# FFN up-projections: the weights' high part times the high and low activations as one product of 512 columns, halves added afterwards

## The reference

```python
def conv_gated_mlp(hn, w_up, conv_w, conv_b, w_down):        # FFN 0 and 1
    u = causal_dwconv(hn @ w_up, conv_w, conv_b)
    gate, val = jnp.split(u, 2, axis=-1)
    return (jax.nn.silu(gate) * val) @ w_down
...
f = (jax.nn.silu(h @ w_ffn_gate[l]) * (h @ w_ffn_up[l])) @ w_ffn_down[l]   # FFN 2
```

## Time and profile before

| | |
|---|---|
| median of 3 runs | 1277.9 us (1277.18 to 1284.03) |
| profiled execution | 1283.02 us, its span 1281.2 us |
| PE busy | 1201.9 us, 94% |
| PE weight loads | 1084.9 us, 85% |
| DVE busy | 721.3 us, 56% |
| ACT busy | 705.4 us, 55% |
| POOL busy | 883.3 us, 69% |
| granted TensorE clock, mean | 0.987 |

### The profile page before, as it was taken

How to read it: one execution, slowest core, us unless ns; L and a number is a source line. 1 busy time by engine, 2 the same in 40 slices (tenths; PEclk the granted TensorE clock), 3 DMA queues, 4 the chain that set the end, 5 groups by cost and what they waited for, 6 DMA issues and landing times.

```text
span 1281.2 us, 23414 instructions
## 1 busy us (share of the span) xinstructions
PE 1201.9 (94%) x8140; PEld 1084.9 (85%) x8140; DVE 721.3 (56%) x1483; ACT 705.4 (55%) x1317; POOL 883.3 (69%) x372
## 2 busy tenths in 40 slices
PE   5888899997899999799999999899999999999997
PEld 3887799876899999688899999788789887999996
DVE  4557736636466666854566666449335634434444
ACT  4766557655355555565565555665456445544442
POOL 3854733346598888543688888688778556888882
PEclk9999999999999999999999999999999999999999
DMA  6668622224766666422466666466557335666650
GB/s 228 188 147 152 195 83 84 76 76 147 224 183 195 191 187 199 145 83 66 148 184 194 191 188 194 139 208 183 164 163 218 128 114 150 179 186 187 185 165 33
DMA packets 61063, 203.46 MB, mean 159 GB/s; under 512 B 6320, under 2 KB 12592, under 8 KB 60864
## 3 DMA queue, kind: packets, MB, share of 16 engines
q1 hardware_dynamic: 53280, 192.96, 49.4%
q10 hardware_dynamic: 7712, 9.52, 3.7%
HBM read 198.26 MB, written 4.19 MB: 158 GB/s over the span
## 4 chain that ended last, share of the span: by engine, by line
PE 81%; DVE 8%; ACT 3%; issue 3%; POOL 1%; ACTq 1%; DVEq 0%; POOLq 0%
PE bank L180 19%; PE bank L181 18%; PE bank L182 18%; PE solve L182 5%; PE solve L181 5%; PE solve L180 5%; DVE xlo L324 1%; ACTq L1333 1%; POOL wlo L167 1%; PE bank L838 0%; ACT whi L163 0%; ACT xhi L318 0%; DVE area L733 0%; PE bank L1691 0%; DVE root_tmp L1247 0%
## 5 line engine op out<-in xcount | busy, mean ns | idle before, releaser
L167 POOL TENSOR_TENSOR wlo<-raw,whi 128x1024 fp32r<-128x1024 f32 x364 | 878.1, 2436 | 375.4 <-ACT whi L163 373.9
L163 ACT ACTIVATE whi<-raw 128x1024 fp32r<-128x1024 f32 x364 | 381.4, 1055 | 147.2 <-PE bank L182 131.5
L180 PE MATMUL bank<-xhi,whi 128*128 128x256 f32 x928 | 271.7, 293 | 14.0 <-DVE xlo L324 8.6
L181 PE MATMUL bank<-xlo,whi 128*128 128x256 f32 x928 | 265.8, 286 | 0.0
L182 PE MATMUL bank<-xhi,wlo 128*128 128x256 f32 x928 | 265.6, 286 | 0.0
L180 PEld LDWEIGHTS bank<-xhi,whi 128*128 128x128 f32 x928 | 181.1, 195 | 20.1 <-DVE xlo L324 10.0
L180 PE MATMUL bank<-whi,xhi 128*128 128x512 f32 (+2 forms) x456 | 178.4, 391 | 7.1 <-issue 4.0
L181 PEld LDWEIGHTS bank<-xlo,whi 128*128 128x128 f32 x928 | 181.2, 195 | 1.1
L182 PEld LDWEIGHTS bank<-xhi,wlo 128*128 128x128 f32 x928 | 181.1, 195 | 0.0
L182 PE MATMUL bank<-whi,xlo 128*128 128x512 f32 (+2 forms) x456 | 174.2, 382 | 0.0
L181 PE MATMUL bank<-wlo,xhi 128*128 128x512 f32 (+2 forms) x456 | 174.1, 382 | 0.0
(11 more groups left out here) (416 smaller groups left out, 1735.1 us busy)
## 6 DMA issues: line engine op xcount, KB each, us to landing
raw<-in_stream SPq DMA_DIRECT2D x364, 512.0 KB, 3.6
band_scratch<-band ACTq DMA_DIRECT2D x1, 3072.0 KB, 35.1
area<-band_scratch ACTq DMA_DIRECT2D x2, 1024.0 KB, 11.8
resid<-in_x SPq DMA_DIRECT2D x2, 512.0 KB, 5.4
scr<-in_row_b_gate ACTq DMA_DIRECT2D x1, 1024.0 KB, 4.6
out<-resid SPq DMA_DIRECT2D x4, 256.0 KB, 2.0
tab<-in_tabs ACTq DMA_DIRECT2D x1, 640.0 KB, 6.9
area<-in_row_final ACTq DMA_DIRECT2D x1, 512.0 KB, 5.6
```

The source lines that it names most:

```text
L163: act.activation(whi[:, n.s, :], raw[:, n.s, :], ACT.Copy).then_inc(hi_ready, 1)
L167: pool.tensor_tensor(wlo[:, n.s, :], raw[:, n.s, :], whi[:, n.s, :].bitcast(F32), ALU.subtract).then_inc(lo_ready, 1)
L180: nc.tensor.matmul(out_ap, a_hi, b_hi, start=start, stop=False)
L181: nc.tensor.matmul(out_ap, a_hi, b_lo, start=False, stop=False)
```

## The change

For the FFN up-projections the two products that use the weights' high part become one matmul of 512 columns: `xhi` and `xlo` now lie in one tensor `xparts`, and the matmul streams the 256 high and the 256 low columns of one slot. High times high lands in columns 0 to 255 of the bank, high times low in columns 256 to 511. The third product, low times high, is added to columns 0 to 255 as before. A new copy on ACT brings columns 256 to 511 to SBUF (`ffn_low`, one buffer for gate and one for value), and a new addition on DVE adds it to columns 0 to 255, before the scaling. ACT's refill of the unit moves ahead of the first tap and behind the new copy. All three FFNs are changed, `two_still` for their first tiles too; everything else keeps its three matmuls.

```diff
-        xhi = sb("xhi", [P, 16, SEQ], F32R)
-        xlo = sb("xlo", [P, 16, SEQ], F32R)
+        xparts = sb("xparts", [P, 2, 16, SEQ], F32R)
+        xhi, xlo = xparts[:, 0], xparts[:, 1]
...
+        def beside(bank, n, w, slot, start, stop):
+
+            nc.tensor.matmul(bank[:], whi[:, n.s, w], xparts[:, :, slot, :], start=start, stop=False)
+            return nc.tensor.matmul(bank[:, 0:SEQ], wlo[:, n.s, w], xhi[:, slot, :], start=False, stop=stop)
...
-                    weights_still(pe, ffn_unit(f, j, i, what), [ps[4 + j % 2 * 2 + half][:, 0:SEQ]], KD, 0)
+                    n = ffn_unit(f, j, i, what)
+                    pe.wait_ge(lo_ready, n.u + 1)
+                    for k in range(KD):
+                        mm = beside(ps[4 + j % 2 * 2 + half], n, slice(k * P, k * P + P), k, k == 0, k == KD - 1)
+                    mm.then_inc(unit_done, 1)
...
# ffn_act
-                    src = ps[4 + p * 2 + half][:, 0:SEQ]
+                    src, low = ps[4 + p * 2 + half][:, 0:SEQ], ps[4 + p * 2 + half][:, SEQ:512]
+                    act.wait_ge(unit_done, n.u + 1)
+                    if j:
+                        act.wait_ge(s.summed, 2 * (before + tile) + half - 1)
+                    act.activation(ffn_low[:, half, :], low, ACT.Copy).then_inc(s.low, 1)
+                    refill(act, n)
                     if conv or half == 0:
                         act.wait_ge(s.scaled, 2 * (before + tile) + half + 1)
...
-                    refill(act, n)
...
# ffn_dve
-                dve.wait_ge(unit_done, ffn_unit(f, j, i, what).u + 1)
+                dve.wait_ge(s.low, nth)
+                dve.tensor_tensor(bank, bank, ffn_low[:, half, :], ALU.add).then_inc(s.summed, 1)
+                dve.wait_ge(s.summed, nth)
                 dve.tensor_tensor(bank, bank, rbc[:], ALU.mult).then_inc(s.scaled, 1)
```

More of the change, by code:

```diff
@@ L414, in turn_half, with two_still @@
                 mm.then_inc(TR.turned, 1)
-        def two_still(pe, key, units, outs):
+        def two_still(pe, key, units, outs, wide=False):
             for half in range(2):
@@ L423, in two_still @@
                         w = slice(k * P, k * P + P)
-                        mm = three(o, whi[:, n.s, w], wlo[:, n.s, w], xhi[:, k, :], xlo[:, k, :], k == 0, k == KD - 1)
+                        if wide:
+                            mm = beside(o, n, w, k, k == 0, k == KD - 1)
+                        else:
+                            mm = three(o, whi[:, n.s, w], wlo[:, n.s, w], xhi[:, k, :], xlo[:, k, :], k == 0, k == KD - 1)
                         if k == KD - 1:
@@ L452, in norm_dve @@
                     dve.tensor_scalar(scr[:, t, cols], resid[:, t, cols], r, None, ALU.mult).then_inc(TR.ready, 1)
-        FS = sems("ffn", "scaled first tap conv silu act hi lo")
-        ffn_g, _o = carve(AREA - 6 * SEQ, 2, SEQ)
+        FS = sems("ffn", "low summed scaled first tap conv silu act hi lo")
+        ffn_low, _o = carve(AREA - 8 * SEQ, 2, SEQ)
+        ffn_g, _o = carve(_o, 2, SEQ)
         ffn_v, _o = carve(_o, 2, SEQ)
@@ L561, in ffn_dve, with scaled @@
             s, key, before = FS, FKEY[f], NF * f
-            def scaled(j, i, half, what):
-                bank = ps[4 + j % 2 * 2 + half][:, 0:SEQ]
-                dve.wait_ge(unit_done, ffn_unit(f, j, i, what).u + 1)
+            def scaled(j, i, half):
+                bank, nth = ps[4 + j % 2 * 2 + half][:, 0:SEQ], 2 * (before + j + 4 * i) + half + 1
+                dve.wait_ge(s.low, nth)
+                dve.tensor_tensor(bank, bank, ffn_low[:, half, :], ALU.add).then_inc(s.summed, 1)
+                dve.wait_ge(s.summed, nth)
                 dve.tensor_tensor(bank, bank, rbc[:], ALU.mult).then_inc(s.scaled, 1)
@@ L573, in tile_of @@
                         nth = 2 * (before + tile) + half + 1
-                        scaled(j, i, half, what)
+                        scaled(j, i, half)
                         dve.wait_ge(s.first, nth)
@@ L587, in tile_of @@
                 else:
-                    scaled(j, i, 0, "gate")
-                    scaled(j, i, 1, "val")
+                    scaled(j, i, 0)
+                    scaled(j, i, 1)
                     dve.wait_ge(s.scaled, 2 * (before + tile) + 2)
```

2 lines of the change are left out of this document (1 added, 1 removed).

## The result

| | before | after |
|---|---|---|
| median | 1280.97 us (4 runs beside it, 1277.18 to 1285.24) | 1308.15 us (4 runs, 1304.6 to 1311.18) |
| ratio after to before | | 1.021, 95% interval 1.0159 to 1.0261 |
| profiled execution, span | 1283.02, 1281.2 us | 1304.6, 1302.8 us |
| granted TensorE clock, mean | 0.987 | 0.983 |

What follows compares the result with a forecast made beforehand. The prediction took PE as the bound before, and POOL's subtractions with DVE's waiting product as the bound of FFN 0 and 1 after: 16.9 + 15.8 + 3.4 - 3.4 = +32.7 us, from 1277.9 to 1310.6 us, range 1294 to 1320.

Steps and rivals of the forecast that it cites:

- The loop: FFN 0 and 1: product always inside POOL's third subtraction, 9.08 us a tile against PE's 8.33; +16.9 and +15.8 us.
- The signs to look for: FFN 0 and 1: POOL in threes, 7.32 us plus 1.76 idle; product over 1 us, flo 0.43; PE waiting.
- Rival (1): FFN 0 and 1: product precedes POOL's third subtraction, PE stays the bound; all stages gain, 1267.3 us; chance 0.12.
- rival (2): FFN 0 and 1: POOL holds up the product in only some tiles, mean 8.7 us a tile, 1297 us; chance 0.16.
- POOL's subtraction: FFN 0 and 1: 2.44 us each, from six in 14.60 us; three end at 7.32 us.
- the link from the addition to the scaling: DVE in each half of a tile: scaling waits 0.15 us for its own engine's addition.
- the chain without POOL: FFN 0 and 1: dependent DVE and ACT work would need 8.4 us a tile, already more than PE's.
- The clock: Last down-projections of FFN 0 and 1: half clock after PE's idleness loses 1.7 us each, +3.4 us (0 to 5.5).
- FFN 2: FFN 2: PE stays the bound at 8.33 us a tile and gains 42 x 0.08 = 3.4 us (0 to 3.5).
- the pair: PE's up-projections: one 512-column matmul at 229 ns plus one 256-column matmul at 119.6 ns.
- The sum: Whole kernel: 16.9 + 15.8 + 3.4 - 3.4 = +32.7 us, median 1277.9 to 1310.6 us.
- One sign: FFN 0 and 1: PE waits on L580 at each up-projection from the middle of the stage.

## Why the prediction was right, and where it was off

**The loop.** The main step, that the product falls into POOL's third subtraction in every tile and so sets the pace of FFN 0 and 1, is confirmed from both sides: with ACT's and DVE's part alone the whole loss is there, and with the product's wait taken away FFN 0 and 1 together are back at 400.2 us, against 400.8 before and 427.9 after. The signs to look for were in the trace: runs of three with 1.76 or 1.84 idle, the product over 1 us from tile 3 on (0.4 to 1.0 in tiles 0 to 2), flo at 0.42. In groups by line, DVE of after (us, mean ns of one, idle before), to be read against the earlier trace rows:

```profile
L604 DVE TENSOR_TENSOR area<-area 128x256 f32<-128x256 f32 x44 | 60.8, 1382 | 5.1 <-ACT area L557 0.8
L614 DVE TENSOR_TENSOR flo<-area,fhi 128x256 fp32r<-128x256 f32 x66 | 54.8, 830 | 33.8 <-ACT fhi L561 33.8
L583 DVE TENSOR_TENSOR bank<-bank,area 128x256 f32<-128x256 f32 x66 | 28.3, 429 | 60.4 <-ACT area L544 60.4
```

flo went from a mean of 1636 to 830 ns, and the addition costs 429 ns, as its nearest row said. Rival (1), that PE stays the bound, and rival (2), a lock in part, did not come: from tile 3 on every tile of FFN 0 and 1 is locked.

**Its size.** 9.08 us a tile was 0.17 too much. The term that was mis-sized is POOL's subtraction, taken at 2.44 us, a sixth of a run of 14.60. In after three take 7.12, 2.37 each, with no DVE product slipped in between two of them as in every second tile before; in the kernel with the gate through PSUM it is 7.13 too, with the product beside it. Taken one by one in the trace of before, the subtractions of the run that starts at 438.49 follow each other 2.36, 2.37, 2.55, 2.56 and 2.38 us apart. The two long ones are those at whose start a DVE instruction with two SBUF inputs got in between: the product (442.71 to 443.53, the subtraction starts at 443.21) and flo (it ends at 446.08, the subtraction starts at 445.76). 18 tiles by 0.17 are 3.1 us a stage. The prediction had 194.2 us from the copy of `rbc` to the end of the last flo; it was 190.4 in FFN 0 and 190.7 in FFN 1, so +13.2 and +12.3 instead of +16.9 and +15.8. The rest, 0.6 and 0.4 us, lies in the written-out tiles. Two more terms were off and did not count, since the product still fell into the third subtraction. It asked 6.04 us behind POOL's start and not 6.4: the link from the addition to the scaling was taken at 0.15 us and measured 0.04 (487.13 + 0.43 to 487.60). And the chain without POOL, taken at 8.4 us and thus above PE's, is 8.0: without the wait PE would have stayed the bound.

**The clock.** 1.7 us for each stage was right as a loss of PE's and wrong on the path in one of two. The last down-projection of FFN 0, PE's timeline and the windows over it (granted clock third from the end):

```profile
521.76 0.80 PE L180 MATMUL bank<-whi,fhi 128*128 128x512 f32 x1 [5.71 <-DVE flo L614]
522.35 0.63 PE L181 MATMUL bank<-wlo,fhi 128*128 128x512 f32 x1
522.78 0.63 PE L182 MATMUL bank<-whi,flo 128*128 128x512 f32 x1
...
526.07 0.60 PE L418 MATMUL solve<-tab,resid 128*128 128x128 f32 x4
```

```profile
518.00:522.00 4.00, 0.24 (x1) 0.24 (x2) 3.05 (x5) 1.36 (x3) 2.51 (x2) 0.51 0.72 230
522.00:526.00 4.00, 4.00 (x12) 3.00 (x13) 4.00 (x7) 1.76 (x4) 3.73 (x2) 0.64 0.43 131
```

After 5.71 us of idleness the granted clock is 0.51, its half level of 1.2 GHz, and matmuls start 0.43 us apart instead of 0.23, until 524.9. From the first of them to the transposes it is 526.07 - 521.76 = 4.31 us. But before it was 4.26 as well, in the trace of before:

```profile
515.87 1.09 PE L413 MATMUL solve<-tab,resid 128*128 128x128 f32 x8 [1.21 <-DVE resid L403]
```

against a first start at 511.61. There the transposes wait 1.21 us for DVE, which is busy with a clearing and two small copies for the next stage, and PE's slow 1.4 us fit into that: after's transposes have no such wait. The prediction had the same transposes follow and overlooked that they wait for DVE anyway. In FFN 1 no such work stands there. PE's first and last row of this stretch in after:

```profile
825.19 0.80 PE L180 MATMUL bank<-whi,fhi 128*128 128x512 f32 x1 [5.75 <-DVE flo L614]
...
829.65 1.03 PE L418 MATMUL solve<-tab,resid 128*128 128x128 f32 x8
```

and in before:

```profile
802.87 0.50 PE L180 MATMUL bank<-whi,fhi 128*128 128x512 f32 x1
...
805.75 1.03 PE L413 MATMUL solve<-tab,resid 128*128 128x128 f32 x8
```

4.46 us, against 805.75 - 802.87 = 2.88 before: 1.6 us, all of it on the path. So the term is 0 + 1.6 instead of 3.4.

**FFN 2.** It gained 2.3 us, not 3.4. A pair of matmuls was to take 229 + 120 = 349 ns. PE's timeline in FFN 2 of after, from the first matmul of a tile's up-projections to the first of the down-projection:

```profile
1187.19 0.39 PE L186 MATMUL bank<-xparts,whi 128*128 128x512 f32 x1
...
1188.94 0.40 PE L186 MATMUL bank<-xparts,whi 128*128 128x512 f32 x1
1189.18 0.28 PE L187 MATMUL bank<-xparts,wlo 128*128 128x256 f32 x1
1189.30 0.40 PE L186 MATMUL bank<-xparts,whi 128*128 128x512 f32 x1
...
1192.83 0.40 PE L180 MATMUL bank<-whi,fhi 128*128 128x512 f32 x1
```

The 16 pairs take 1192.83 - 1187.19 = 5.64 us, 352.5 ns each: 236 from the wide to the narrow one, 117 back. Before, 16 times three of 256 columns took 488.70 - 482.95 = 5.75 us, and 359.5 ns each in the mean of 16 tiles of FFN 2. A pair saves 7.0 ns where the prediction counted 10, a unit 0.056 us where it counted 0.08. The term that was mis-sized is the pair, priced as if each matmul kept the pace that it has among equal neighbours. The Trainium skill (TensorE: Matmul & The Clock Gate, Wait — 56ns, not 53.3ns?) has a fixed cost of 2.5 ns a matmul, so 2.5 saved by each pair. The measured 7.0 lies between that and the 10, nearer to the 10. 42 units by 0.056 are 2.4 us, which is all that FFN 2 gained: the tile went from 8.50 to 8.39 us.

**The sum.** Loop +13.2 and +12.3, clock 0 and +1.6, FFN 2 -2.3: +24.8, against a difference of 27.2 between the medians and 21.6 between the spans (24.6 without the first copy). Predicted was +32.7, 7.9 too much. The median itself was missed by 2.5 us only, and part of that is luck: the prediction stood on 1277.9 us for before, and the runs beside after gave 1280.97. Another part is that the medians lie 2.4 us further apart than the stages of the traces account for, which no run here explains.

**One sign was misread.** PE was to wait for L580, the taps, at each up-projection from the middle of the stage on. Its waits in after, grouped (us, times, longest):

```profile
PE bank L180 <- DVE flo L614: 17.1, 4, 5.8
PE bank L180 <- POOL wlo L167: 9.1, 26, 2.7
```

PE is held at down-projections instead, until POOL's third subtraction has the unit ready, for 0.2 to 0.4 us idle each time, from 391.24 on in FFN 0 and from 721.42 on in FFN 1 (the 2.7 us lie behind FFN 1, not in the loop). Until then PE lives on its lead and keeps its 8.39 us a tile. The four waits for flo are those before the last two down-projections of both stages, 2.8 and 5.7 us each time, where some 5 before each were predicted. All of them belong to the same loop, so the time is the same.

## What to carry to other kernels

Here a DVE instruction with both inputs in SBUF cost what POOL's current subtraction had left, so price added DVE work by where it pushes the next such instruction against POOL's rhythm and not by its own 0.43 us. Where the two engines lock, putting one input into PSUM (here by the ACT instruction that writes it anyway) removed that instruction's wait altogether, which pays provided that the bank is not thereby held for an engine that needs it. And a stall priced at the end of a stage has to be followed one step beyond: the same loss of clock cost 1.6 us in one FFN and nothing in the other.

## What the runs showed of the hardware

A product with both inputs in SBUF took 1.36, 2.34, 2.46 or 2.62 us, according to what was left of POOL's subtraction, and 0.42 with one input in PSUM in the middle of one. In after it ended 0.28 us behind POOL's. Where it got in between two subtractions, it took 0.82 us, and the subtraction behind it was 0.19 us longer than the others. The Trainium skill (SBUF — State Buffer, SBUF: two separate sides) calls the pair of ports that DVE and GpSimd share an exclusive lock, held for a whole instruction, which a DVE instruction needs in a 2-port mode, or with two SBUF inputs against a GpSimd instruction that reads SBUF, as the subtraction does; the trace agrees, with the waits above. There is also a case with one input, a copy of 16 elements a partition from SBUF to SBUF, in the trace of before:

```profile
512.55 2.01 DVE L1477 COPY area<-small 128x16 f32<-128x16 f32 x1
514.47 0.17 DVE L1477 COPY area<-small 128x16 f32<-128x16 f32 x1
```

2.01 us against 0.17 for the next one, while POOL was in a subtraction that began at 512.12 and took 2.4; in after the same copy took 1.98. That this copy ran in such a mode is not shown by any run here.

Matmuls of 512 and 256 columns in turn cost 352.5 ns a pair, three of 256 columns 359.5, and whether the 512 columns are one run or two made no difference. One ACT instruction that issues a DMA took between 4.7 and 7.5 us in the eleven traces, whose kernels do not differ in it.
